# Routed experts on Trainium2: the round counts of an expert group as one packed word, extra rounds as nested branches, packed expert lists

## The chip, the cores and the metric

The kernel runs on one core of one Trainium2 chip. The metric is the device time of one execution in microseconds. Three runs of the kernel before took 1653.17, 1653.27 and 1659.96 us; the median is 1653.27 us. The profiled execution took 1655.41 us, of which the profile's span covers 1653.7 us; the rest lies around it.

## The reference, cut to what matters

Two transformer blocks run one after the other on 256 tokens of width 1024. Each ends in routed experts, and only these are touched by the change. The first has 32 experts, two for each token; the second has 64 experts, eight for each token. All experts have width 256. All weights are float32.

```python
# first block: 4 groups of 8 experts; the best group, then its best two experts
g_top = jnp.argmax(g_logits, axis=-1)
e_in = jnp.take_along_axis(e_logits, g_top[:, None, None], axis=1)[:, 0]
e_val, e_loc = lax.top_k(e_in, TOP_K)
e_w = jax.nn.softmax(e_val, axis=-1) * g_w[:, None]
# for each expert, on the tokens that chose it:
hb = jax.nn.silu(xb @ w_gate[e]) * (xb @ w_up[e])
return (hb @ w_down[e]).astype(F32) * wt[:, None]

# second block: the best 4 of 8 groups, then the best 8 experts of these
g, u = jnp.split(jnp.einsum('td,edf->tef', tc, w_gu), 2, axis=-1)
routed = jnp.einsum('tef,efd->td', jax.nn.silu(g) * u * gc[..., None], w_down)
```

Which tokens an expert gets, and how many, is known only when the kernel runs.

## The kernel before, in words

**Groups, rounds and jobs.** Experts are sorted by their number of tokens, and four of them form a group: two from the busy end of the order and two from the other end. The first layer has NQ = 8 groups, the second 16. A job is 32 tokens of one expert, and a round is four jobs, which lie in four blocks of 32 rows of TensorE. Each group has one round in which every expert of it has a job. If a pair of the group has an expert with more than 32 tokens, extra rounds follow in which only this pair has jobs, two each: n2 extra rounds for the first pair, n3 for the second. The counts come from the routing, which VectorE works out on the chip.

**A round on TensorE** (`one` in `moe_pe`): the gate/up matmuls (L321, two instructions of each kind for each call, since float32 takes two), the gathering of tokens for the next round by one-hot matrices (`pick`, L280), the sum of the last round's outputs into the accumulators (`combine`, L289), the columns of the slots (L270), two transposes (L333), a second `pick`, and the down matmuls (L344). ScalarE and VectorE take silu, product, copies and the next one-hot matrices (`onehot`, L214 to L223) between these. In the first round of a group, TensorE waits for the four experts' gate/up weights (L297) and down weights (L301).

**The order of rounds on TensorE** is written out by hand, group by group (I call one group's share of this a turn). Register loads (`value_load`) read small integers from the list `lst` in memory on the chip. L102 (`window_end`) loads the number of rounds up to this group. After the group's first round, L353 loads n2, a branch (L356) goes past the extra rounds if it is zero, and otherwise a loop of four passes (L357) runs the round where the pass is below n2 (L358). The same follows for n3, with a load of n3 at L353 and one more of n2 at L355. A register load shows in the trace as TENSOR_LOAD, FUSED_REGOPS and SEQ_ASSERT, a branch as COMPARE_BRANCH, all on TensorE's sequencer (PEldq).

```python
for i in range(m.NQ):
    g = window_end(pe, m, i - 1) if i else 0
    one(g, i, (0, 1, 2, 3), True)
    for h, which in enumerate(((0, 1, 0, 1), (2, 3, 2, 3))):
        n = pe.value_load(...L_N + 2 * i + h...)
        if h: g = pe.value_load(...L_N + 2 * i...) + g
        with pe.If(n > 0):
            with pe.Fori(0, T // (2 * JOB)) as r:
                with pe.If(n > r): one(r + (g + 1), i, which, False)
```

**The other engines** run the rounds as a loop over a common number of rounds (`rounds`). SyncE issues the weight loads (`moe_sp`): seven slots hold gate/up weights, 2 MB an expert, and four hold down weights, 1 MB an expert. A slot is loaded anew when the rounds of its group are done.

**Lists.** `route_lists_dve` and `route_lists_pe` make six lists of 80 entries, one entry for each round: the experts of its four jobs, and where the jobs of each pair start (L459 to L466). TensorE turns them into rows by six transposes (L387), and VectorE copies 480 numbers to `lst` as integers (L469). `onehot` reads six numbers for each round.

Of the kernel before, what the change touches and what calls it, by code (L numbers as in the profile page):

```python
# [19 lines left out]
I32 = mybir.dt.int32  # L20
# [6 lines left out]
P = 128  # L27
# [183 lines left out]
def moe_dve(dve, m, ev, ps):  # L211
    def onehot(g):

        first = [dve.value_load(m.lst[0:1, bass.ds(g + (4 + h) * JOBS, 1)], min_val=0, max_val=2 * T - JOB) for h in range(2)]  # L214
        for j in range(PER):
            e = dve.value_load(m.lst[0:1, bass.ds(g + j * JOBS, 1)], min_val=0, max_val=m.E - 1)
            dve.tensor_tensor(m.oneh[:, :, JOB * j:JOB * j + JOB],  # L217
                              m.iota[:, bass.ds(first[j // 2], JOB)].unsqueeze(1).to_broadcast([P, TT, JOB]),
                              m.pos[:, :, bass.ds(e, 1)].to_broadcast([P, TT, JOB]), ALU.is_equal)
# [46 lines left out]
def moe_pe(pe, m, ev, ps):  # L266
# [44 lines left out]

    def one(g, i, which, first):
        at = [PER * i + w for w in which]
# [12 lines left out]
        if not isinstance(g, int):  # L326
# [21 lines left out]

    for i in range(m.NQ):
        g = window_end(pe, m, i - 1) if i else 0  # L350
        one(g, i, (0, 1, 2, 3), True)
        for h, which in enumerate(((0, 1, 0, 1), (2, 3, 2, 3))):
            n = pe.value_load(m.lst[0:1, m.L_N + 2 * i + h:m.L_N + 2 * i + h + 1], min_val=0, max_val=T // (2 * JOB))  # L353
            if h:
                g = pe.value_load(m.lst[0:1, m.L_N + 2 * i:m.L_N + 2 * i + 1], min_val=0, max_val=T // (2 * JOB)) + g  # L355
            with pe.If(n > 0):  # L356
                with pe.Fori(0, T // (2 * JOB)) as r:  # L357
                    with pe.If(n > r):  # L358
                        one(r + (g + 1), i, which, False)
# [7 lines left out]
def route_lists_pe(pe, m, ev, ps):  # L367
# [18 lines left out]
    for i in range(6):  # L386
# [4 lines left out]
def route_lists_dve(dve, m, ev, ps):  # L391
# [38 lines left out]
    dve.tensor_copy(m.lst[0:1, m.L_N:m.L_N + 2 * NQ], m.n[0:1].rearrange("o i h -> o (i h)"))  # L430
# [28 lines left out]
    dve.scalar_tensor_tensor(m.job[:, 0:2], m.dif, third, m.abcd[:, 0:2], ALU.mult, ALU.add)  # L459
    dve.scalar_tensor_tensor(m.job[:, 2:4], m.dif, back, m.abcd[:, 2:4], ALU.mult, ALU.add)  # L460
    dve.tensor_tensor(k, r, k, ALU.subtract)
    dve.drain()
    dve.tensor_scalar(m.job[:, 4:5], k, 2.0 * JOB, -float(JOB), ALU.mult, ALU.add)
    dve.tensor_scalar(m.job[:, 5:6], k, 2.0 * JOB, None, ALU.mult)
    dve.drain()
    dve.tensor_scalar(m.job[:, 4:6], m.job[:, 4:6], ext, float(2 * T - JOB), ALU.mult, ALU.min)  # L466
# [6 lines left out]
def build_program(nc, A, out):  # L473
    ctx = contextlib.ExitStack()
    with ctx:
# [99 lines left out]
        def moe_buffers(prefix, E, most):  # L575
# [10 lines left out]
            m.lst = take("lst", [1, JOBS * 6 + E + 3 * m.NQ]).bitcast(I32)  # L586
            m.L_X, m.L_END, m.L_N = JOBS * 6, JOBS * 6 + E, JOBS * 6 + E + m.NQ
# [6 lines left out]
            m.total, m.end, m.past, m.begun, m.junk = (take(n, [P, m.NQ]) for n in ("total", "end", "past", "begun", "junk"))  # L594
            m.st = take("st", [P, 8])
            m.abcd, m.dif, m.job = take("abcd", [P, PER]), take("dif", [P, 2]), take("job", [P, 6])
# [1517 lines left out]
```

## Time and profile before

| | |
|---|---|
| median of three runs | 1653.27 us |
| the profiled execution | 1655.41 us |
| its span | 1653.7 us |
| TensorE busy | 1278.0 us (77%) |
| VectorE busy | 533.2 us (32%) |
| ScalarE busy | 321.2 us (19%) |
| read from HBM | 399.15 MB, 242 GB/s over the span |
| routed experts, first layer | about 340 to 585 us |
| routed experts, second layer | about 1050 to 1645 us |

How to read it: the busy time of an engine counts only its work, not its sequencer's register loads, branches and waits. In the views, PE is TensorE's matmuls, PEld its weight loads, PEldq and PEq its sequencer, DVE VectorE, ACT ScalarE. "Issue" is time in which an engine waited for nothing that the profile shows, such as its own sequencer. The granted clock of TensorE was 0.875 of its full rate on average.

### The profile page before, as it was taken

The numbers are of one execution on the slowest core, as the hardware profiler recorded it, in microseconds if no ns is written. First come the engines' busy times: TensorE is split into PE (matmuls) and PEld (weight loads), VectorE is DVE, ScalarE is ACT, GpSimd is POOL, SyncE is SP. The second block draws the span as 40 slices with busy tenths as digits, with TensorE's granted clock in tenths as the row PEclk, the third lists the DMA queues.
The fourth block names the chain that finished last, engine by engine and source line by source line (L and its number), as shares of the span: only waits on it lengthen the run. The fifth ranks groups of instructions, "written<-read, shape, count | busy, mean of one in ns | idle before, by whom it ended". The sixth has DMA issues, their size and how long they took to land.

```text
span 1653.7 us, 23849 instructions
## 1 busy us (share of the span) xinstructions
PE 1278.0 (77%) x8269; PEld 675.7 (41%) x8269; DVE 533.2 (32%) x1556; ACT 321.2 (19%) x566; POOL 44.5 (3%) x90
## 2 busy tenths in 40 slices
PE   6998867468746664999479977698999978888645
PEld 4752243333322332864254435344444433344322
DVE  0004132422121113599644414332233332222122
ACT  2114431411100123101352214011111111111000
POOL 1001100200000000000000003000000000000000
PEclk9997767679877877999789997799999999999877
DMA  7548700398999685244000923675888887778993
GB/s 263 184 159 299 251 16 1 118 388 329 421 419 419 270 301 198 96 160 152 0 1 8 348 69 142 255 292 227 326 348 344 350 358 306 286 304 325 427 423 148
DMA packets 87950, 402.32 MB, mean 243 GB/s; under 512 B 10944, under 2 KB 19572, under 8 KB 59136
## 3 DMA queue, kind: packets, MB, share of 16 engines
q1 hardware_dynamic: 86608, 399.70, 61.7%
q8 instruction: 111, 1.82, 0.4%
q10 hardware_dynamic: 816, 0.52, 0.2%
q14 instruction: 31, 0.25, 0.0%
q0 software_dynamic: 384, 0.03, 0.0%
HBM read 399.15 MB, written 1.07 MB: 242 GB/s over the span
## 4 chain that ended last, share of the span: by engine, by line
PE 43%; DMA 8%; issue 4%; DVE 2%; ACT 1%; DVEq 1%; PEldq 1%; PEld 1%; ACTq 0%; SPq 0%
PE ps L1965 17%; PE ps L321 13%; DMA ring<-in_w_exp_gu 5%; PE ps L344 4%; PE ps L280 4%; PE ps L289 2%; DMA big<-in_w_exp_gu 1%; DMA big<-mod 1%; PE ps L797 1%; PE ps L270 0%; PE ps L333 0%; ACT big L1661 0%; DVE big L1780 0%; DVE big L1778 0%; PE ps L2043 0%
## 5 line engine op out<-in xcount | busy, mean ns | idle before, releaser
L321 PE MATMUL ps<-ring,big 128*32 128x512 f32 x2128 | 306.2, 650 | 144.0 <-issue 61.2
L321 PEld LDWEIGHTS ps<-ring,big 128*32 128x32 f32 x2128 | 86.2, 119 | 332.4 <-issue 332.4
L1965 PE MATMUL ps<-ring,big 128*128 128x512 f32 x464 | 202.0, 594 | 2.3 <-ACTq L777 1.1
L321 PE MATMUL ps<-big 128*32 128x512 f32 x304 | 131.0, 657 | 19.7 <-DMA ring<-in_w_up 12.9
L344 PE MATMUL ps<-big 128*32 128x512 f32 x1216 | 138.4, 595 | 0.0
L1965 PEld LDWEIGHTS ps<-ring,big 128*128 128x128 f32 x464 | 87.3, 190 | 110.4 <-issue 107.2
L280 PEld LDWEIGHTS ps<-big 128*128 128x128 bf16 x1920 | 115.4, 99 | 34.6 <-issue 31.9
L280 PE MATMUL ps<-big 128*128 128x128 bf16 x1920 | 125.4, 221 | 1.5 <-ACT big L192 1.5
L201 ACT ACTIVATE big<-ps 128x256 f32<-128x256 f32 x38 | 14.6, 386 | 502.0 <-PE ps L321 502.0
L1766 DVE SCALAR_TENSOR_TENSOR big<-big 128x256 f32<-128x256 f32 x240 | 105.6, 481 | 9.0
L243 DVE TENSOR_TENSOR big<-big,ps 128x256 f32<-128x256 f32 x38 | 16.1, 423 | 276.7 <-ACT big L201 276.7
L217 DVE TENSOR_TENSOR big<-iota,big 128x64 f32 x168 | 37.9, 225 | 202.2 <-issue 202.2
L289 PE MATMUL ps<-parts,slot_tok 128*128 128x512 f32 x304 | 82.6, 415 | 12.4 <-issue 6.8
L192 ACT COPY big<-ps 128x512 f32<-128x512 f32 x80 | 47.0, 588 | 220.2 <-PE ps L280 220.2
L797 PE MATMUL ps<-ident,big 128*128 128x128 f32 x144 | 30.4, 399 | 76.4 <-DVEq L1793 24.8
L1965 PE MATMUL ps<-big,ring 128*128 128x256 f32 x320 | 71.8, 388 | 0.9 <-ACTq L777 0.9
L289 PEld LDWEIGHTS ps<-parts,slot_tok 128*128 128x128 f32 x304 | 56.4, 196 | 24.7 <-issue 14.2
L1965 PEld LDWEIGHTS ps<-big,ring 128*128 128x128 f32 x320 | 62.2, 195 | 9.9 <-ACTq L777 1.1
L344 PEld LDWEIGHTS ps<-big 128*32 128x32 f32 x1216 | 35.7, 110 | 72.2 <-issue 68.2
L797 PEld LDWEIGHTS ps<-ident,big 128*128 128x128 f32 x144 | 27.7, 214 | 80.5 <-DVEq L1240 18.7
L245 DVE COPY big<-ps 128x256 f32<-128x256 f32 x38 | 16.2, 426 | 117.3 <-PE ps L333 117.3
L1346 PE MATMUL ps<-big,ring 128*96 128x256 f32 (+1 forms) x224 | 48.8, 379 | 0.0
(435 smaller groups left out, 1287.6 us busy)
## 6 DMA issues: line engine op xcount, KB each, us to landing
ring<-in_w_exp_gu SPq DMA_DIRECT2D x55, 2048.0 KB, 17.6
big<-in_w_exp_down SPq DMA_DIRECT2D x64, 1024.0 KB, 9.0
big<-in_w_down SPq DMA_DIRECT2D x32, 1024.0 KB, 14.8
ring<-in_w_in SPq DMA_DIRECT2D x15, 2048.0 KB, 8.0
ring<-in_w_gate SPq DMA_DIRECT2D x28, 1024.0 KB, 16.6
ring<-in_w_up SPq DMA_DIRECT2D x28, 1024.0 KB, 19.5
ring<-in_w_ada SPq DMA_DIRECT2D x12, 2048.0 KB, 8.0
big<-in_w_exp_gu SPq DMA_DIRECT2D x9, 2048.0 KB, 18.0
```

Source lines behind the costliest of these rows:

```text
L192: act.copy(m.xsT[:, 4 * r:4 * r + 4, :].rearrange("p a b -> p (a b)"), ps[:, BT, :]).then_inc(ev(m.p + "Te"), 1)
L217: dve.tensor_tensor(m.oneh[:, :, JOB * j:JOB * j + JOB], m.iota[:, bass.ds(first[j // 2], JOB)].unsqueeze(1).to_broadcast([P, TT, JOB]), m ...
L243: dve.tensor_tensor(m.hid, m.sg, ps[:, BG, 256:512], ALU.mult).then_inc(ev(m.p + "hid"), 1)
L245: dve.tensor_copy(m.hidT.rearrange("p a b -> p (a b)"), ps[:, BG, 0:256])
L280: last = pe.matmul(ps[:, BT, c * P:(c + 1) * P], m.tok3[:, part * TT + t, f], m.oneb[:, t, :], start=(part + t == 0), stop=(part == 2 and ...
L289: last = pe.matmul(ps[:, ACC + 2 * t + n, :], m.S[:, t * P:(t + 1) * P], part[:, n * 512:(n + 1) * 512], start=False, stop=True, skip_grou ...
L321: last = pe.matmul(ps[rows, BG, :], m.xsT[:, k, rows], m.gu(m.gu_slot(at[j]), k), start=(k == 0), stop=(k == KC - 1), skip_group_check=True)
L344: last = pe.matmul(ps[rows, BD + n, :], m.hidT[:, k, rows], m.dring[:, at[j] % DOWN_SLOTS, k * D + n * 512:k * D + n * 512 + 512], start=( ...
L797: last = pe.transpose(ps[:, bank0 + c // 2, (c % 2) * T + t * P:(c % 2) * T + (t + 1) * P], src[:, t, c * P:(c + 1) * P], ident[:])
L1346: last = pe.matmul(ps[0:m, g % 4, 0:n], lhs(k), rhs(k), start=(k == 0), stop=(k == KC - 1))
L1766: dve.scalar_tensor_tensor(convT[:, c, :], uT[:, c, k:k + T], dwc[:, c, k:k + 1], convT[:, c, :], ALU.mult, ALU.add)
L1965: last = pe.matmul(bank, lhs(k), rhs(k), start=(k == 0 and start), stop=(k == kk - 1))
```

## The change

1. **Extra rounds on TensorE.** The first extra round of the first pair stands in line within `If(n2 > 0)`; only further ones are in a loop, from pass 1 on, within a second `If(n2 > 1)`. The second pair keeps its loop of four passes, within `If(n3 > 0)`.
2. **One packed word.** n2, n3 and the first round's number of a group are packed into one word (`L_W`), from which TensorE takes all three by shifts and masks. The word of the next group is loaded within this group's first round, behind `combine`. The loads at L102, L353 and L355 go. The word is built on VectorE by two more operations, with a drain and a copy.
3. **Packed lists.** The four experts of a round are packed into one number and the two starts into another: two lists instead of six, two transposes instead of six, and a copy of 160 numbers. `onehot` loads two numbers and takes the rest by shifts and masks on VectorE's sequencer.

```diff
@@ moe_dve, onehot
-        first = [dve.value_load(m.lst[0:1, bass.ds(g + (4 + h) * JOBS, 1)], min_val=0, max_val=2 * T - JOB) for h in range(2)]
+        packed = dve.value_load(m.lst[0:1, bass.ds(g, 1)], min_val=0, max_val=2 ** 24 - 1)
+        chunks = dve.value_load(m.lst[0:1, bass.ds(g + JOBS, 1)], min_val=0, max_val=255)
         for j in range(PER):
-            e = dve.value_load(m.lst[0:1, bass.ds(g + j * JOBS, 1)], min_val=0, max_val=m.E - 1)
+            e = (packed >> (6 * j)) & (m.E - 1)
+            first = ((chunks >> (4 * (j // 2))) & 15) * JOB
@@ moe_pe
+    def word(i):
+        return pe.value_load(m.lst[0:1, m.L_W + i:m.L_W + i + 1], min_val=0, max_val=2 ** 13 - 1)
     def one(g, i, which, first):
...
             combine()
+        if first and i + 1 < m.NQ:
+            following = word(i + 1)
         pe.wait_ge(ev(m.p + "hid"), g + 1)
...
+    following = word(0)
+    more = T // (2 * JOB)
     for i in range(m.NQ):
-        g = window_end(pe, m, i - 1) if i else 0
+        now = following
+        g, n2, n3 = now & 127 if i else 0, (now >> 7) & 7, now >> 10
         one(g, i, (0, 1, 2, 3), True)
-        for h, which in enumerate(((0, 1, 0, 1), (2, 3, 2, 3))):
...
+        with pe.If(n2 > 0):
+            one(g + 1, i, (0, 1, 0, 1), False)
+            with pe.If(n2 > 1):
+                with pe.Fori(1, more) as r:
+                    with pe.If(n2 > r):
+                        one(r + (g + 1), i, (0, 1, 0, 1), False)
+        with pe.If(n3 > 0):
+            with pe.Fori(0, more) as r:
+                with pe.If(n3 > r):
+                    one(r + n2 + (g + 1), i, (2, 3, 2, 3), False)
@@ route_lists_pe
-    for i in range(6):
+    for i in range(2):
@@ route_lists_dve
-    dve.tensor_copy(m.lst[0:1, m.L_N:m.L_N + 2 * NQ], m.n[0:1].rearrange("o i h -> o (i h)"))
+    dve.scalar_tensor_tensor(m.words, m.n[:, :, 1], 8.0, m.n[:, :, 0], ALU.mult, ALU.add)
...
+    dve.scalar_tensor_tensor(m.words, m.words, 128.0, m.begun, ALU.mult, ALU.add)
...
+    dve.drain()
+    dve.tensor_copy(m.lst[0:1, m.L_W:m.L_W + NQ], m.words[0:1, :])
...
-    dve.tensor_copy(m.lst[0:1, 0:6 * JOBS], ps[0:1, BT, 0:6 * JOBS])
+    dve.tensor_copy(m.lst[0:1, 0:2 * JOBS], ps[0:1, BT, 0:2 * JOBS])
```

## Rows read from the trace of the kernel before

**Rows 1.** Page: engines busy (us, share, instructions); DMA queue (packets, MB, share).

```profile
PE 1278.0 (77%) x8269; PEld 675.7 (41%) x8269; DVE 533.2 (32%) x1556; ACT 321.2 (19%) x566; POOL 44.5 (3%) x90
...
q8 instruction: 111, 1.82, 0.4%
```

**Rows 2.** Waits view, TensorE: who waited on what: us in total, times, longest.

```profile
PE ps L321 <- issue: 68.0, 21, 8.2
...
PE ps L321 <- DMA ring<-in_w_up: 45.2, 4, 12.9
```

**Rows 3.** Timeline of TensorE, 540:560 us; then the source view of L297, 555:559 us.

```profile
558.11 2.79 PE L321 MATMUL ps<-ring,big 128*32 128x512 f32 x12 [12.73 <-DMA ring<-in_w_up]
...
L297 PEldq EVENT_SEMAPHORE  x3: 51/51/51, 556.2 to 558.0; - x3
```

**Rows 4.** Windows view: us, busy time by engine (x), PEclk, DMA share, GB/s.

```profile
410.00:560.00 150.00, 92.53 (x802) 42.14 (x798) 27.99 (x95) 11.24 (x20) 0.00 (x0) 0.80 1.01 419
...
1163.00:1525.00 362.00, 315.94 (x3010) 154.68 (x2999) 107.29 (x367) 42.75 (x76) 0.00 (x0) 0.96 0.81 325
...
1215.00:1217.00 2.00, 1.23 (x12) 0.13 (x4) 0.61 (x4) 0.27 (x1) 0.00 (x0) 1.00 0.00 0
```

**Rows 5.** Source views, whole span: duration ns min/median/max, first and last start us.

```profile
L356 PEldq COMPARE_BRANCH  x48: 70/1033/6436, 359.4 to 1637.5; - x48
...
L357 PEldq COMPARE_BRANCH  x52: 86/224/242, 398.5 to 1522.7; - x52
```

**Rows 6.** Source views of L357, L353, 1213:1219 us; timeline of TensorE, 1213:1222.

```profile
L357 PEldq COMPARE_BRANCH  x4: 86/224/238, 1213.6 to 1215.8; - x4
...
L357 PEldq ALU_OP  x4: 32/36/36, 1213.5 to 1215.8; - x4
...
L353 PEldq TENSOR_LOAD <-big x1: 302/302/302, 1216.0 to 1216.0; - x1
...
1218.85 3.64 PE L321 MATMUL ps<-ring,big 128*32 128x512 f32 x32 [2.62 <-issue]
```

**Rows 7.** Source view of L356, in seven short windows of one jump each.

```profile
L356 PEldq COMPARE_BRANCH  x1: 332/332/332, 1180.5 to 1180.5; - x1
...
L356 PEldq COMPARE_BRANCH  x1: 5861/5861/5861, 1358.4 to 1358.4; - x1
...
L356 PEldq COMPARE_BRANCH  x1: 1876/1876/1876, 424.7 to 424.7; - x1
...
L356 PEldq COMPARE_BRANCH  x1: 6436/6436/6436, 1602.4 to 1602.4; - x1
...
L356 PEldq COMPARE_BRANCH  x1: 4236/4236/4236, 1579.7 to 1579.7; - x1
...
L356 PEldq COMPARE_BRANCH  x1: 4741/4741/4741, 1610.2 to 1610.2; - x1
...
L356 PEldq COMPARE_BRANCH  x1: 3371/3371/3371, 1637.5 to 1637.5; - x1
```

**Rows 8.** Chain of what ended last, 1180:1192 us: start us, us, what.

```profile
1184.71 1.39 issue
```

**Rows 9.** Chains of 1360:1376 and 1286:1300 us; timeline of TensorE, 1353:1368.

```profile
1365.40 8.43 PE ps L321 x64
...
1290.81 7.07 PE ps L321 x64
...
1365.40 1.07 PE L321 MATMUL ps<-ring,big 128*32 128x512 f32 x2 [8.08 <-issue]
```

**Rows 10.** Timeline of TensorE 332:342 us; TensorE waits; source view of L214, 333:341.

```profile
332.44 0.96 PE L387 MATMUL ps<-ident,big 80*1 80x80 f32 x6 [5.56 <-DVEq L467]
...
PE ps L270 <- DVEq L223: 13.7, 2, 7.0
...
L214 DVEq TENSOR_LOAD <-big x2: 315/437/559, 334.2 to 335.1; - x2
```

More of the change, by code:

```diff
@@ L212, in onehot @@
     def onehot(g):
-        first = [dve.value_load(m.lst[0:1, bass.ds(g + (4 + h) * JOBS, 1)], min_val=0, max_val=2 * T - JOB) for h in range(2)]
+        packed = dve.value_load(m.lst[0:1, bass.ds(g, 1)], min_val=0, max_val=2 ** 24 - 1)
+        chunks = dve.value_load(m.lst[0:1, bass.ds(g + JOBS, 1)], min_val=0, max_val=255)
         for j in range(PER):
-            e = dve.value_load(m.lst[0:1, bass.ds(g + j * JOBS, 1)], min_val=0, max_val=m.E - 1)
+            e = (packed >> (6 * j)) & (m.E - 1)
+            first = ((chunks >> (4 * (j // 2))) & 15) * JOB
             dve.tensor_tensor(m.oneh[:, :, JOB * j:JOB * j + JOB],
-                              m.iota[:, bass.ds(first[j // 2], JOB)].unsqueeze(1).to_broadcast([P, TT, JOB]),
+                              m.iota[:, bass.ds(first, JOB)].unsqueeze(1).to_broadcast([P, TT, JOB]),
                               m.pos[:, :, bass.ds(e, 1)].to_broadcast([P, TT, JOB]), ALU.is_equal)
@@ L325, in one @@
         pick(0)
-        if not isinstance(g, int):
+        if not (isinstance(g, int) and g == 0):
             pe.wait_ge(ev(m.p + "S"), g)
@@ L347, in one @@
             last.then_inc(ev(m.p + "down"), 1)
+    following = word(0)
+    more = T // (2 * JOB)
     for i in range(m.NQ):
-        g = window_end(pe, m, i - 1) if i else 0
+        now = following
+        g, n2, n3 = now & 127 if i else 0, (now >> 7) & 7, now >> 10
         one(g, i, (0, 1, 2, 3), True)
-        for h, which in enumerate(((0, 1, 0, 1), (2, 3, 2, 3))):
[L353 to L359, printed above, removed]
+        with pe.If(n2 > 0):
[8 more added lines that the diff above has]
+                    one(r + n2 + (g + 1), i, (2, 3, 2, 3), False)
     total = all_rounds(pe, m)
@@ L458, in route_lists_dve @@
     dve.drain()
-    dve.scalar_tensor_tensor(m.job[:, 0:2], m.dif, third, m.abcd[:, 0:2], ALU.mult, ALU.add)
-    dve.scalar_tensor_tensor(m.job[:, 2:4], m.dif, back, m.abcd[:, 2:4], ALU.mult, ALU.add)
+    dve.scalar_tensor_tensor(m.job4[:, 0:2], m.dif, third, m.abcd[:, 0:2], ALU.mult, ALU.add)
+    dve.scalar_tensor_tensor(m.job4[:, 2:4], m.dif, back, m.abcd[:, 2:4], ALU.mult, ALU.add)
     dve.tensor_tensor(k, r, k, ALU.subtract)
     dve.drain()
-    dve.tensor_scalar(m.job[:, 4:5], k, 2.0 * JOB, -float(JOB), ALU.mult, ALU.add)
-    dve.tensor_scalar(m.job[:, 5:6], k, 2.0 * JOB, None, ALU.mult)
+    two = m.job4.rearrange("p (h j) -> p h j", j=2)
+    dve.scalar_tensor_tensor(m.dif, two[:, :, 1], 64.0, two[:, :, 0], ALU.mult, ALU.add)
+    dve.tensor_scalar(k, k, 7.0, 34.0, ALU.min, ALU.mult)
     dve.drain()
-    dve.tensor_scalar(m.job[:, 4:6], m.job[:, 4:6], ext, float(2 * T - JOB), ALU.mult, ALU.min)
+    dve.scalar_tensor_tensor(m.job[:, 0:1], m.dif[:, 1:2], 4096.0, m.dif[:, 0:1], ALU.mult, ALU.add)
+    dve.tensor_scalar(m.job[:, 1:2], k, -1.0, ext, ALU.add, ALU.mult)
     dve.drain().then_inc(ev(m.p + "jobs"), 1)
     dve.wait_ge(ev(m.p + "jobrows"), 1)
-    dve.tensor_copy(m.lst[0:1, 0:6 * JOBS], ps[0:1, BT, 0:6 * JOBS])
+    dve.tensor_copy(m.lst[0:1, 0:2 * JOBS], ps[0:1, BT, 0:2 * JOBS])
     dve.drain().then_inc(ev(m.p + "list"), 1)
@@ L585, in moe_buffers @@
             m.gu_data = lambda slot: ring[:, slot, 0:4096] if slot < RING else gu7
-            m.lst = take("lst", [1, JOBS * 6 + E + 3 * m.NQ]).bitcast(I32)
-            m.L_X, m.L_END, m.L_N = JOBS * 6, JOBS * 6 + E, JOBS * 6 + E + m.NQ
+            m.lst = take("lst", [1, JOBS * 2 + E + 2 * m.NQ]).bitcast(I32)
+            m.L_X, m.L_END, m.L_W = JOBS * 2, JOBS * 2 + E, JOBS * 2 + E + m.NQ
             m.pos = take("pos", [P, TT, E])
@@ L594, in moe_buffers @@
             m.total, m.end, m.past, m.begun, m.junk = (take(n, [P, m.NQ]) for n in ("total", "end", "past", "begun", "junk"))
+            m.words, m.job4 = take("words", [P, m.NQ]), take("job4", [P, PER])
             m.st = take("st", [P, 8])
-            m.abcd, m.dif, m.job = take("abcd", [P, PER]), take("dif", [P, 2]), take("job", [P, 6])
+            m.abcd, m.dif, m.job = take("abcd", [P, PER]), take("dif", [P, 2]), take("job", [P, 2])
             m.own = take("own", [P, PER])
```

1 line of the change is left out of this document (added).

## The prediction

> **What bounds the kernel now.** I read the page first, then TensorE's waits, then the two routed-expert stages (340 to 590 us and 1050 to 1640 us), the only places that the change touches. The page shows TensorE as the busiest engine, 77% [rows 1]. The waits view tells what its idle time ends on: gate/up matmuls (L321) wait 68.0 us on "issue", that is on TensorE's own sequencer, and in four turns 45.2 us on a weight DMA [rows 2]. The DMA label says what came last, not what took long. In the turn that starts at 558.11 us TensorE stood idle for 12.73 us, but its sequencer reached the three waits at L297 only at 556.2 us and had passed the last at 558.0 us [rows 3]: at most 1.8 us were the DMA, the rest was the sequencer.
>
> The stages have two regimes. A turn of the group loop with no extra round is one round, about 17 us of matmuls, against 12 MB of weights; there the DMA share is 1.01 at 419 GB/s (410 to 560 us), and DMA sets the pace. From 1163 to 1525 us, where turns have two rounds each, the DMA share is 0.81 and TensorE is busy for 315.94 of 362 us [rows 4]: TensorE sets the pace, and its idle time counts in full.
>
> Which turns have extra rounds: the loop over them (L357) was entered 13 times (52 loop ends, four to an entry) [rows 5]. By the shortest jumps at L356 (70 to 84 ns, body entered) these are turn 1 of the first layer (n2 = 1) and, in the second, turn 0 (n3 = 1), turn 1 (n2 = 2) and turns 2 to 11 (n2 = 1). Seven turns of the first layer and the last four of the second have none.
>
> **What stands between two rounds.** Turn 5 of the second layer, after its extra round (last matmul issued at 1213.5 us): four loop ends at L357 from 1213.6 us, with the tests at L358 between them; the load of L353 at 1216.0 us and that of L355, each 0.302 us and its register work, 0.65 to 0.72 us in all; a jump over the n3 body, 0.38 us; the load of L102, again 0.65; some 0.4 us of waits; first matmul at 1218.85 us [rows 6]. TensorE had 2.6 us queued when the sequencer left the round, so 5.3 us of sequencer give 2.62 us of idle [rows 6].
>
> **The jump is the dear part.** COMPARE_BRANCH at L356 took 70 to 6436 ns [rows 5], and its place decides. After an extra round the jump took 0.33 to 0.45 us in seven of the ten turns 2 to 11, and 5.8 to 6.0 us in three [rows 7]. In turns without an extra round two jumps follow each other, and the second took 4.2 to 4.7 us every time under full DMA load; the first took 1.9 to 6.4 us [rows 7]. With DMA idle it is less: 3.37 us at 1637.5 us [rows 7]. I read that as code coming from memory: TensorE's instruction queue moves 111 packets, 1.82 MB, 16.4 KB each [rows 1]; for the 28,454 instructions that I count in its program that is 64 B each, 256 to a packet. A round is 316 matmuls and weight loads, some 322 instructions, 1.26 packets. Sorted by their place within a packet, the jumps that don't follow another one fall apart: over one stretch of a quarter to half a packet all are under 0.5 us, over the next all but one, with DMA idle, are 5.7 to 6.4 us; just behind a packet boundary they shrink with the distance (6.0, 4.2, 3.6, 1.9 us). So the next packet is asked for when the one before it is entered, arrives 5.5 to 6.4 us later under DMA load and 3 to 4 us later with DMA idle, and a jump beyond it pays that in full. The bill can come later as well: after a short jump the round at 1181.97 us stops at 1184.71 us for 1.39 us within its matmuls [rows 8]. The Trainium skill says the same in words (Runtime: NRT & Kernel Launch, Instruction fetch mechanics): prefetch is sequential, and a taken branch out of the current two pages waits for a DMA. It speaks against this change, which lengthens the code by a body in each turn.
>
> **The change, part by part (times for the profiled execution, 1655.4 us).**
> 1. Sequencer work removed in a turn with n2 = 1: the loop's empty passes 2.4 us (1213.6 to 1216.0), two loads 1.37, the load of L102 0.64: 4.4 us [rows 6]. Added: four or five register operations; the nearest row is the loop's ALU_OP at 32 to 36 ns, 0.1 us with the gap behind it [rows 6]: 0.4 us (0.2 to 0.8).
> 2. The packed word is loaded within the round, behind combine: 0.66 us in which combine's 8 matmuls (1.9 us) are queued. I cost it at nothing; uncovered it is 24 x 0.66 = 16 us.
> 3. Jumps in such a turn. Before: one, over one body; mean of the ten (7 x 0.38 + 3 x 5.9) / 10 = 2.0 us. After: the extra round runs in line, then a jump over the loop (one body), and at once a jump over the n3 body. The first I leave at 2.0 us. The second is the kind that pairs show: 4.2 to 4.7 us behind 1.3 us of loads, so 5.6 to 6.1 us from the landing of the first; with DMA idle 3 to 4. Here DMA is nearly idle between the end of the round and SyncE's next loads (share 0.00 in 1215 to 1217 us) [rows 4], so about half the turns see each: 4.8 us, bounds 0.35 and 6.1. Net of parts 1 and 3: -4.4 + 0.4 + 4.8 = +0.8 us.
> 4. Idle above 5 us costs clock besides: behind 8.08 us of idle at 1365.40 us the gate/up matmuls take 8.43 us, behind 2.6 us (1290.81) 7.07 [rows 9]: 1.4 us. Three of ten turns have that now, six or so would; and a round that starts late in a packet stops within it. Together +0.7 us. So +1.5 us a turn, ten turns: **+15 us**.
> 5. Second layer, turn 0: +0.5. Turn 1: one empty pass less and no load; -2. Turns 12 to 14: a jump over two bodies and one over one, about 12.5 us beside 13.5 now, but DMA sets the end: 0. Turn 15: DMA idle, loads gone: -1.
> 6. First layer, turn 0: two jumps, 5.0 us in all now, over two bodies and one under full load 6 each; less two saved loads and a test: +4. Turn 1: 0. Turns 2 to 6 lose up to 3 us of sequencer against a slack of some 2 us at the DMA gate [rows 3], and DMA has a backlog then [rows 4]: 0. Turn 7: -0.7.
> 7. Lists: two transposes for six (0.96 us to 0.3), a copy of 160 numbers for 480, two register loads for six ahead of the first picks (about 0.6 us each by the row of L214, against some 0.35 us a job of shifts) [rows 10]; one drain and two small operations more, 0.4 us. TensorE waits for this once a layer (13.7 us in two) [rows 10]: -2 a layer, bounds 0 and -3. In all other rounds VectorE's shorter lists lie beside matmuls and are worth nothing. If they were late, TensorE would show more waits for L223 than these two.
>
> Sum: first layer +4 - 0.7 - 2 = +1.3; second -2 + 0.5 - 2 + 15 - 1 = +10.5; in all +12. Against the median (1653.3, 2.1 us below the profiled execution) that is **1665 us**.
>
> **Rivals.**
> - Jumps come cheap. If a jump in line costs 0.35 us wherever it goes, each of the ten turns gains 4.4 - 0.4 - 0.4 = 3.6 us, 36 in all, and with turn 1, the starts and ends some 44: 1610 us. For it: 7 of 10 single jumps were short. Against: not one second jump under load was. It decides if the second costs less than 4 us. The Trainium skill (Advanced Engine Details and Errata, Control Flow Timing) gives about 108 ns for a compare-and-branch, which would bring this case; no long row here agrees. Chance 0.17.
> - Code comes in strict order and always under load: every skipped packet costs 6 us. Then the pair costs about 11 us for 6.8, +45 in the ten turns, and turns without extra rounds, which now skip 2.5 packets at once, pass the DMA's pace by 3 us in some eight: 1665 + 45 + 24 = 1734. For it: the packets moved (111) equal the whole program, skipped bodies included. Against: one jump beyond the next packet costs no more than one packet. Chance 0.16.
> - The two halves cancel: the second jump lies nearer 3.5 us, since DMA is idle just then. Then the ten turns give 0 +- 8: 1650 to 1660. Chance 0.22.
> - My case, +8 to +40: 0.45.
>
> **Numbers.** Slower by over 0.5% (8 us, about what a measurement can tell here): 0.60; within: 0.19; faster: 0.21 (the first rival and an edge of the third). The range 1632 to 1706 leaves out most of the first rival and of the second.
>
> **What would show it.** Right: L356's successors show two long jumps in a row in turns 2 to 11, 3 to 6 us for the second; the instruction queue moves about 28 packets more; busy times hardly change; TensorE's idle time in turns 2 to 11 grows from 46 us (362 - 316) [rows 4]. Wrong: second jumps under 1 us, or a wait at the new word load. The weakest step is how long a packet takes while DMA is between two loads.

## The result, and the profile after

The changed kernel takes 1674.27 us (median; 1665.59 to 1684.64), the kernel before 1656.49 us in the same session (1644.65 to 1662.24). The ratio is 1.0118, 95% interval 1.0091 to 1.0144: slower by 17.8 us. Forecast were 1665 us and +12. A ratio leaves out executions more than 1.5% above their kernel's fastest; only the last kernel below had any, three of ten, its traced one of 1670.92 us among them. The profiled execution of the changed kernel took 1668.87 us, 1667.1 of it span.

The page of the changed kernel, engines busy and the queue that carries code; these answer [rows 1]:

```profile
PE 1273.8 (76%) x8261; PEld 673.3 (40%) x8261; DVE 532.9 (32%) x1562; ACT 321.4 (19%) x566; POOL 44.5 (3%) x90
...
q8 instruction: 134, 2.20, 0.5%
```

TensorE does the same work in nearly the same busy time. What grew is the code that its queue moved, by 23 packets. Its waits (who waited on what: us in total, times, longest) answer [rows 2] and [rows 10]; L321 has become L328, L270 L272, L223 L225:

```profile
PE ps L328 <- issue: 111.2, 19, 15.5
PE ps L328 <- DMA ring<-in_w_up: 47.8, 4, 13.5
...
PE ps L272 <- DVEq L225: 9.9, 2, 5.1
```

Idle time in front of gate/up matmuls that ends on TensorE's own sequencer went from 68.0 to 111.2 us. The wait for the first round's lists went from 13.7 to 9.9 us.

The windows view of turns 2 to 11 of the second layer (us, busy time by engine, PEclk, DMA share, GB/s), first the kernel before, cut at the first gate/up matmul of turn 2 and of turn 12, then the changed kernel, cut in the same way:

```profile
1141.85:1525.66 383.81, 334.80 (x3161) 163.14 (x3162) 112.67 (x384) 45.00 (x80) 0.00 (x0) 0.95 0.82 330
```

```profile
1141.96:1543.75 401.79, 338.10 (x3160) 163.69 (x3161) 113.59 (x381) 45.01 (x80) 0.00 (x0) 0.92 0.79 320
```

Ten turns take 17.98 us more: 14.7 us are idle time (401.79 - 338.10 = 63.7 against 49.0), 3.3 us are slower matmuls at a lower granted clock. Of the idle time, 18.4 us more lie between rounds (61.33 against 42.95), and the stops within rounds fell from 6.0 to 2.1 us (sums of the gaps in the timelines). The source views of the two jumps in these turns (duration in ns, min/median/max): L366, out of the first half's block behind the in-line round, and L370, over the second half's.

```profile
L366 PEldq COMPARE_BRANCH  x10: 369/3370/4700, 1172.7 to 1533.5; - x10
...
L370 PEldq COMPARE_BRANCH  x10: 3128/5165/6377, 1176.6 to 1537.4; - x10
```

There are two long jumps in a row where there was one. One by one, with the place in a packet of 256 instructions at which L366 stands (counted in the program; its zero is fitted here and is checked below):

| turn | 2 | 3 | 4 | 5 | 6 | 7 | 8 | 9 | 10 | 11 | mean |
|---|---|---|---|---|---|---|---|---|---|---|---|
| place of L366 | .83 | .95 | .07 | .19 | .31 | .44 | .56 | .68 | .80 | .92 | |
| L366, us | 3.65 | 3.81 | 3.54 | 3.20 | 2.45 | 1.13 | 0.43 | 0.37 | 4.70 | 3.63 | 2.69 |
| L370, us | 5.67 | 5.53 | 6.08 | 3.35 | 3.13 | 3.27 | 4.80 | 4.55 | 6.38 | 5.79 | 4.85 |

Both jumps span 1.28 packets. From 0.72 on a jump lands two packets further, and waits; behind a boundary it lands in the next packet, which has only just been asked for, and the wait shrinks with the distance, to nothing at 0.6. In the timeline the end of turn 2 looks like this (start us, us, instruction, idle time before it and its releaser):

```profile
1182.80 1.04 PE L328 MATMUL ps<-ring,big 128*32 128x512 f32 x1 [7.32 <-issue]
```

7.32 us of idle time, where the same place had 2.63 us before.

That the jumps wait for code can be read directly, since the traces hold the times of the code queue's packets. The DMA view of the changed kernel in the time of two jumps (queue: packets that started, MB, share), first L366 at the end of turn 2 (1172.74 to 1176.39 us), then L370 behind it (1176.56 to 1182.23 us):

```profile
q1 hardware_dynamic: 29, 0.21, 13.8%
q8 instruction: 1, 0.02, 2.2%
```

```profile
q1 hardware_dynamic: 250, 1.92, 94.0%
q8 instruction: 1, 0.02, 1.1%
```

The code packet starts 1.0 us after the first jump and 3.4 us after the second, takes 1.3 and 1.0 us, and each jump ends 1.4 us after it has landed. The second jump is longer because SyncE's weight loads run by then. From 300 us on, the twelve traces of this text have 336 branches on TensorE that last over 2.2 us. A code packet lands within every one of them, and the branch ends 1.3 to 2.0 us after the last one (in 316 of them 1.3 to 1.6 us). Of the 802 branches under 0.6 us, 780 have none.

### The profile page after: what moved, and what is told of

Same layout as the page of the kernel before. It is cut to its first block, busy times and chain, and to the rows that moved or that the text cites. A ratio compares the mean times of both kernels' runs of the same rounds, so it can differ in the third digit from the quotient of the medians.

```text
span 1667.1 us, 23346 instructions
## 1 busy us (share of the span) xinstructions
PE 1273.8 (76%) x8261; PEld 673.3 (40%) x8261; DVE 532.9 (32%) x1562; ACT 321.4 (19%) x566; POOL 44.5 (3%) x90
## 4 chain that ended last, share of the span: by engine, by line
PE 44%; issue 6%; DMA 5%; DVE 3%; ACT 2%; DVEq 1%; PEld 1%; SPq 0%; PEldq 0%; ACTq 0%
PE ps L1985 16%; PE ps L328 13%; PE ps L353 5%; PE ps L282 4%; DMA ring<-in_w_exp_gu 3%; PE ps L291 3%; DMA big<-in_w_exp_gu 1%; PE ps L272 1%; PE ps L817 1%; PE ps L342 0%; DMA big<-mod 0%; SPq L1564 0%; DMA posi<-in_positions 0%; DVE big L1800 0%; DVE big L1798 0%
## 5 line engine op out<-in xcount | busy, mean ns | idle before, releaser
L328 PE MATMUL ps<-ring,big 128*32 128x512 f32 x2128 | 312.2, 670 | 154.6 <-issue 95.8
L328 PEld LDWEIGHTS ps<-ring,big 128*32 128x32 f32 x2128 | 88.2, 122 | 349.3 <-issue 346.3
L328 PE MATMUL ps<-big 128*32 128x512 f32 x304 | 132.2, 662 | 28.9 <-issue 15.5
L353 PE MATMUL ps<-big 128*32 128x512 f32 x1216 | 138.4, 595 | 0.0
L353 PEld LDWEIGHTS ps<-big 128*32 128x32 f32 x1216 | 35.7, 110 | 72.2 <-issue 68.2
L328 PEld LDWEIGHTS ps<-big 128*32 128x32 f32 x304 | 30.9, 121 | 53.4 <-issue 52.5
```

What stands on the lines that cost most here:

```text
L328: last = pe.matmul(ps[rows, BG, :], m.xsT[:, k, rows], m.gu(m.gu_slot(at[j]), k), start=(k == 0), stop=(k == KC - 1), skip_group_check=True)
L353: last = pe.matmul(ps[rows, BD + n, :], m.hidT[:, k, rows], m.dring[:, at[j] % DOWN_SLOTS, k * D + n * 512:k * D + n * 512 + 512], start=( ...
```

## The experiments

Ten kernels ask three things: which part of the change costs, what a long jump waits for, and whether it can be had without. Ratios are to the kernel before, which ran beside each.

**Only the packed lists on VectorE.** The kernel before with this part alone:

```diff
-        first = [dve.value_load(...) for h in range(2)]
+        packed = dve.value_load(m.lst[0:1, bass.ds(g, 1)], ...)
+        chunks = dve.value_load(m.lst[0:1, bass.ds(g + JOBS, 1)], ...)
-    for i in range(6):
+    for i in range(2):
         last = pe.transpose(...)
```

> Kernel before with the packed expert lists on VectorE alone; TensorE's loads, loops and branches are as before, its code is 16 instructions shorter. Theory (a jump pays for a code packet that has not come): the list stages give 2 us each, 4 us in all; besides, all of the second layer's code moves by 0.06 packet, so that after extra rounds the long jumps of 5 to 6 us stand in turns 7 and 8 and no longer in turn 9: another 5 us. 9 us faster than before, ratio 0.994. Rival (jumps cost what they cost by the load on the DMA queues, not by their place): long jumps stay in turns 7, 8 and 9, 4 us faster, 0.998.

Measured: 0.9966 (0.9945 to 0.9986), 1647.58 us. The lists bring 5.6 us (2.3 to 9.1). In the traces the stage from the matmuls ahead of the transposes (L382, in the changed kernel L396) to the first pick is 2.07 us shorter in the first layer of the changed kernel, and 1.66 in the second; the interval holds that sum. The long single jumps came at the ends of turns 6, 7 and 8 (5.57, 5.86, 5.73 us), where the kernel before has them at 7, 8 and 9: still three, so no gain there. My count of where they would go was off by one turn.

**Only the in-line copy.** The kernel before with the changed kernel's nested branches, but each count loaded where it is used:

```diff
+        n2 = count(i, 0)
         with pe.If(n2 > 0):
-            (loop over four passes)
+            one(g + 1, i, (0, 1, 0, 1), False)
+            with pe.If(n2 > 1): (loop over three passes)
+        n3 = count(i, 1)
+        n2 = count(i, 0)
         with pe.If(n3 > 0): ...
```

> Kernel before with the in-line copy of the first extra round and the nested branch alone; the counts are loaded as before, lists as before. Theory: in turns 2 to 11 of the second layer the three empty passes go (2.4 us), but a second jump comes, from which the two loads between the jumps hide 1.3 us: first jumps 28 us in all, second ones 32 us, against 20 us of single jumps before, so +40 - 24 = +16 us there, +7 us in the first layer (turn 0 and its DMA), -1 in turn 1: 20 to 25 us slower, ratio 1.013. Rival (the sequencer's work is what counts, a jump is 0.4 us): 10 x 2.0 us faster, ratio 0.988.

Measured: 1.0202 (1.0177 to 1.0227), 1688.82 us, +33 us. The rival, that removed passes are a gain, falls, and the theory gave too little. In turns 2 to 11 (source views) the first jump takes 2.69 us on average and the last 2.89:

```profile
L360 PEldq COMPARE_BRANCH  x10: 371/2994/5376, 1189.8 to 1550.1; - x10
...
L366 PEldq COMPARE_BRANCH  x10: 1682/2919/4362, 1196.5 to 1553.9; - x10
```

Here two loads stand between the jumps, 1.3 us [rows 6], and the second jump is 2.0 us shorter than the changed kernel's 4.85. The loads also lengthen a turn, so the places in the packet differ too.

**Only the word and the lists.** The changed kernel without the copy:

```diff
         with pe.If(n2 > 0):
-            one(g + 1, i, (0, 1, 0, 1), False)
-            with pe.If(n2 > 1):
-                with pe.Fori(1, more) as r:
+            with pe.Fori(0, more) as r:
```

> The changed kernel without the in-line copy: the packed word, read ahead, and the packed lists stay, both pairs have the loop of four passes again, one body each. Theory: each of the ten turns loses two loads and the one of L102 and gains 0.4 us of shifts, -1.6 us; code is as long as before, one jump after an extra round, long (5 to 6 us) in turns 5 and 6 alone by its place; lists -4 us. In all -16 - 5 - 4 = -25 us against before, ratio 0.985. Rival (the word's read ahead costs TensorE within the round): 0.66 us in each of 24 turns back, ratio 0.995. Rival (the in-line copy is no matter): like the changed kernel, 1.01.

Measured: 0.9763 (0.9739 to 0.9787), 1615.73 us. Better than any case expected. So the copy, put on top of this, costs 1.0118 / 0.9763 = 1.036, some 59 us, almost twice the 33 us that it costs alone. The windows view of its turns 2 to 11 says where the unexpected part is:

```profile
1141.69:1492.24 350.55, 325.43 (x3160) 166.19 (x3161) 114.72 (x385) 45.04 (x80) 0.00 (x0) 0.99 0.89 361
```

33.3 us less than before, of which 23.9 us are idle time (25.1 against 49.0) and 9.4 us are faster matmuls at a granted clock of 0.99 instead of 0.95. The second part I had left out. At the ends of these turns the kernel before has three gaps of 8 us and seven of 2.6 to 2.8 us; here six of ten are under 2 us and the longest is 3.9. The windows view of the kernel before shows that even the shorter gaps can cost clock, and need not. These are the first 64 gate/up matmuls behind a gap of 2.71 us and behind one of 2.62 us:

```profile
1254.60:1263.37 8.77, 8.77 (x66) 2.90 (x66) 2.73 (x4) 0.00 (x0) 0.00 (x0) 0.81 1.01 419
1290.81:1297.88 7.07, 7.07 (x65) 2.43 (x66) 2.75 (x4) 0.00 (x0) 0.00 (x0) 1.00 1.01 425
```

**Loops that end at the count.** The same, without the empty passes:

```diff
-            with pe.Fori(0, more) as r:
-                with pe.If(n2 > r):
-                    one(r + (g + 1), i, (0, 1, 0, 1), False)
+            with pe.Fori(0, n2) as r:
+                one(r + (g + 1), i, (0, 1, 0, 1), False)
```

> As e3_word, but the loops run to the count itself, with no empty passes and no test inside. Theory: 2.4 us of empty passes go too, so the jump comes earlier after its packet was asked for and part of it comes back: jumps about 29 us in the ten turns against 20 before, sequencer -40 us, lists -4, turn 1 -3: about -38 us against before, ratio 0.977; long jumps (over 3 us) in turns 3, 4, 9, 10, 11. Rival (empty passes hide the fetch in full): same as e3_word.

Measured: 0.9713 (0.9690 to 0.9736), 1607.92 us. The empty passes took 2.4 us of sequencer in a turn [rows 6], but ten turns gain only 350.55 - 343.16 = 7.4 us by their removal: the jump over the second half's block, 1.45 us on average with them, is 2.67 us without (its places in the packet moved as well). They had covered part of the fetch.

**A gap between the jumps.** The changed kernel with 3.9 us of loads of no use:

```diff
+        for _ in range(6):
+            word(i)
         with pe.If(n3 > 0):
```

> The changed kernel with six more loads of the count word (0.65 us of sequencer each, 3.9 us in all, 21 instructions) between the first half's branch and the second half's, in every turn. Theory (the second jump waits for a packet that arrives at its own time, whatever the sequencer does meanwhile): in the second layer's turns 2 to 11 the second jump falls from 4.86 us to about 1.2 us (each value of the changed kernel less 3.9, not under 0.35), the two together stay, and the time stays within 8 us of the changed kernel's, ratio to before 1.010 to 1.018. Rival (the jump has a price of its own, paid from when it issues): the second jump stays near 4.9 us, each of the 24 turns is 3.9 us longer less what the DMA hides in the first layer and turns 12 to 15, some +45 us, ratio 1.035 to 1.045.

Measured: 1.0372 (1.0333 to 1.0411), 1712.96 us. The time is the rival's, the trace is neither's alone. Two jumps over the second half's block (L372), at the ends of turns 2 and 4, in the source view:

```profile
L372 PEldq COMPARE_BRANCH  x1: 6232/6232/6232, 1189.7 to 1189.7; - x1
...
L372 PEldq COMPARE_BRANCH  x1: 439/439/439, 1279.0 to 1279.0; - x1
```

In six of the ten turns the second jump is 0.34 to 0.50 us: the loads cover its whole wait. These are the turns whose first jump waited (2.89 to 3.36 us), so that the packet behind its landing place was asked for before the gap. In the other four the first jump took 0.36 to 0.45 us and the second, which lands two packets on, 5.75 to 6.74 us: the gap doesn't help, since nothing asks for that packet before the jump. The packet times agree. In the six turns a code packet lands between the two jumps, and none within the second. In the four one lands between them too, but another starts within the second, 3.4 to 4.4 us after its start, beside weight loads:

```profile
q1 hardware_dynamic: 317, 2.34, 94.4%
q8 instruction: 1, 0.02, 1.0%
```

(DMA view, 1189.65 to 1195.88 us.) The loads also lengthen a turn's code and so moved every jump to another place. The windows view of the ten turns:

```profile
1148.38:1570.16 421.78, 345.09 (x3160) 165.03 (x3161) 113.11 (x380) 45.04 (x80) 0.00 (x0) 0.90 0.75 302
```

Against the changed kernel the turns are 20.0 us longer, not 39: 13.0 us of idle time (76.7 against 63.7) and 7.0 us of clock, 0.90 against 0.92. So about two thirds of the added sequencer time lay within waits for code. The rest of the 1.0372 came outside these turns, where I had counted on cover from the DMA. A fixed price of a jump is refuted; my figure for the time was wrong.

**Code moved, nothing else.** The kernel before with one alignment ahead of the second layer's lists:

```diff
+    if m.E == 64:
+        pe.addr_align(256, offset=147, max_nops=0)
     pe.wait_ge(ev(m.p + "jobs"), 1)
```

> The kernel before, with nothing but an alignment of TensorE's code ahead of the second layer's lists, which moves all code behind it by 0.35 of a 256-instruction packet. Theory (a jump of 1.28 packets waits when it starts in the last quarter of a packet, since its landing place is then two packets on): the long single jumps over the second half, which were in turns 7, 8 and 9 (5.8 to 6.0 us), go to turns 2, 3, 10 and 11; turns 4 to 9 show 0.33 to 0.6 us. Time 1650 to 1665 us. Rival (something of turns 7 to 9 itself, such as their experts or the loads under way, makes the jump long): they stay in turns 7, 8 and 9.

Measured in one execution: 1653.84 us. The long jumps left turns 7, 8 and 9, as only the theory says, but went to 5, 6 and 7:

```profile
L356 PEldq COMPARE_BRANCH  x1: 5781/5781/5781, 1285.6 to 1285.6; - x1
...
L356 PEldq COMPARE_BRANCH  x1: 5663/5663/5663, 1327.3 to 1327.3; - x1
...
L356 PEldq COMPARE_BRANCH  x1: 5681/5681/5681, 1368.6 to 1368.6; - x1
...
L356 PEldq COMPARE_BRANCH  x1: 351/351/351, 1409.9 to 1409.9; - x1
```

I had miscounted where the lists stand in the program: the alignment moved the code by 0.75 of a packet, not 0.35. With the right count the jumps at the ends of turns 5, 6 and 7 start at 0.96, 0.84 and 0.72 of a packet, and all others, at 0.61 and below, are short. That needs no fitted zero, since the alignment sets it, and it confirms the one used in the table above.

**Fewer weights beside the code.** The changed kernel, where the second layer loads a quarter of each expert's weights from its second turn on:

```diff
+            if getattr(m2, "light", False):
+                eng.dma_start(m2.gu_data(slot)[:, 0:1024], ...[:, 0:1024]).then_inc(sem, 16)
+                return
```

> The changed kernel, but from its second turn on the second layer loads only a quarter of each expert's gate/up and down weights, so that its result is not the reference's; TensorE's instructions are the same. Theory (a packet of code comes through the same DMA engines, behind weight packets): with the DMA engines mostly idle a packet comes in 3 to 3.5 us, so the second jumps of the second layer's turns 2 to 11 fall from 4.86 to about 3 us and none is over 4, the jumps of turns 12 to 15 from 5.5 to 6.7 down to about 3 us each; those turns, no longer held by loads, fall from 30 to about 23 us. Rival (the wait is a fixed price of a refill, whatever the DMA engines do): second jumps stay at 4.5 to 6 us.

Measured in one execution: 1642.21 us; the DMA share of the ten turns is 0.27 instead of 0.79. The source views of its second jumps in turns 2 to 11, and of both jumps in turns 12 to 15:

```profile
L373 PEldq COMPARE_BRANCH  x10: 2862/3851/4605, 1187.0 to 1528.2; - x10
...
L367 PEldq COMPARE_BRANCH  x4: 3440/3705/3957, 1548.8 to 1620.6; - x4
...
L373 PEldq COMPARE_BRANCH  x4: 3142/3394/3922, 1552.4 to 1624.7; - x4
```

In turns 12 to 15 the pair fell to 3.1 to 4.0 us each; the changed kernel, under full load, has 6.1 to 6.5 and 5.5 to 5.7 us there in turns 12 to 14. In turns 2 to 11 the second jump fell from 4.85 to 3.73 us on average, not to 3, and four were over 4.1 us: weights account for about a quarter of that wait. In two of the four, turns 8 and 9 (4.61 and 4.54 us), the code queue moved two packets within the jump. The ten turns are 22 us shorter (379.57 us).

**A hint for the jump.** The kernel of the fourth experiment, with the jump over the second half's block announced at the head of the extra round:

```diff
             with pe.Fori(0, n2) as r:
+                here = pe.mark_branch_hint_location()
                 one(r + (g + 1), i, (0, 1, 0, 1), False)
-        with pe.If(n3 > 0):
+        pe.br_eq(n3, 0, on_true=name + "_end", on_false=name + "_body").branch_hint(here)
```

> e4_count (the packed word read ahead, loops that end at the count, no in-line copy) with one thing added: at the head of the first half's extra round the code hints that the jump over the second half's block will be taken, some 16 us before that jump. Theory (a jump waits because the packet of its landing place has only just been asked for, or not yet): in the second layer's turns 2 to 11 of e4_count that jump lasted 3.13, 3.89, 3.39, 0.36, 1.09, 1.62, 2.75, 3.25, 3.53 and 3.64 us; with the packet asked for 16 us earlier all ten are 0.3 to 0.6 us. TensorE's idle time between these turns falls from 11 us in all to about 0, and with fewer slow gate/up matmuls the ratio to the kernel before goes from 0.971 to about 0.962. Rival (the jump itself is dear, or the hint does nothing): the jumps stay at 3 us and the ratio at 0.971. Third: the hint fetches a packet that is thrown out again before the jump; then waits of 3 us and more stay, and code traffic grows by some ten packets.

Measured: 0.9706 (0.9661 to 0.9751), 1599.59 us; not told apart from 0.9713. The source views of a jump that lands two packets on, at the end of turn 4, first without the hint and then with it:

```profile
L367 PEldq COMPARE_BRANCH  x1: 3392/3392/3392, 1237.1 to 1237.1; - x1
```

```profile
L370 PEldq COMPARE_BRANCH  x1: 388/388/388, 1231.2 to 1231.2; - x1
```

Without the hint the four jumps from 0.77, 0.83, 0.92 and 0.99 of a packet took 3.4 to 3.9 us; with it the three from 0.79, 0.92 and 0.94 took 0.37 to 0.39. Jumps just behind a boundary waited as before: 2.84 and 2.88 us at 0.22 and 0.21, 3.57 and 3.54 at 0.08 and 0.07. The hint fetches a packet that the order of the code would skip; it does not hasten the next one. The page has 106 packets on the code queue instead of 110. My "all ten" was wrong, and the position in the packet stayed as the thing to set. That is the next experiment.

**Hint and place.** Each turn of the second layer starts at instruction 55 of a packet, so that the hinted jump starts at 0.80:

```diff
         now = following
+        if m.E == 64:
+            pe.addr_align(256, offset=55, max_nops=0)
```

> e5_hint with one thing added: each turn of the second layer starts at instruction 55 of a 256-instruction packet, so that a turn takes 4.00 packets instead of 3.86 and the jump over the second half's block starts at 0.80 of a packet in every turn. In e5_hint that jump lasted 0.37 to 0.39 us where it started at 0.64, 0.79, 0.92 and 0.94 of a packet, and 0.49 to 0.76 at about 0.4 to 0.5, 2.04, 2.88, 2.84 and 3.54 at 0.35, 0.21, 0.22 and 0.07. Theory (position within the packet, with the hint, decides): all ten jumps of turns 2 to 11 last under 0.6 us, the idle time of TensorE between these turns falls from about 7 us in all to under 2, and the ratio to the kernel before is about 0.965. Rival (the waits belong to the turns, not to the place in the packet): long jumps stay in turns 2, 3, 8, 9 and 10 and the ratio at 0.971. Third: the branch over the padding costs more than it gives, 0.3 us and more in each of 16 turns; then the jumps are short and the ratio still 0.970 or above.

(In the text above "0.49 to 0.76 at about 0.4 to 0.5" should read 0.76 us at 0.49.) Measured: 0.9656 (0.9632 to 0.9679), 1593.85 us, the fastest kernel here: by the ratios 57 us under the kernel before and 76 under the changed one. The source view of the hinted jump, then the windows view, turns 2 to 11:

```profile
L372 PEldq COMPARE_BRANCH  x10: 367/378/408, 1158.2 to 1453.5; - x10
```

```profile
1128.06:1456.99 328.93, 319.24 (x3164) 163.27 (x3157) 114.14 (x384) 45.04 (x80) 0.00 (x0) 1.00 0.93 384
```

All ten jumps are short, the clock is full. Idle time is 9.7 us, not the 2 expected; TensorE's waits in this stretch say what holds it now:

```profile
PE ps L328 <- DMA ring<-in_w_exp_gu: 7.1, 8, 1.3
PE ps L353 <- DMA big<-in_w_exp_down: 1.0, 2, 0.5
PE ps L328 <- DMA big<-in_w_exp_gu: 0.5, 1, 0.5
```

In this stretch nothing waits for the sequencer any more; the weights are the bound, at a DMA share of 0.93. Turns 12 to 14 have no extra round and so no hint: their jumps over the second half's block take 7.40 to 7.64 us, against 5.57 to 7.14 without the fixed place.

**Hints in the changed kernel.** Two, both at the head of the in-line copy:

```diff
         with pe.If(n2 > 0):
+            here = [pe.mark_branch_hint_location() for _ in range(2)]
             one(g + 1, i, (0, 1, 0, 1), False)
-            with pe.If(n2 > 1):
+            pe.br_lt(n2, 2, on_true=..., on_false=...).branch_hint(here[0])
...
-        with pe.If(n3 > 0):
+        pe.br_eq(n3, 0, on_true=..., on_false=...).branch_hint(here[1])
```

> The changed kernel with two hints at the head of each in-line copy: that the jump out of the first half's block is taken, and the one over the second half's. Nothing else is changed. In e5_hint a hint took the wait from jumps that land two packets on and from no others. Theory: the first jumps of turns 2, 3, 10 and 11, which land two packets on (3.65, 3.81, 4.70, 3.63 us), fall to about 0.4 us; the second jump of the same turns lands one packet further and still waits some 3 to 6 us; the others stay. That is 14 us of jump time less in four turns, of which some comes back in the second jumps: ratio to before 1.000 to 1.010. Rival (both hinted packets are kept): both jumps are short in all turns, and the ratio falls to 0.98. Second rival: the second hint displaces the first, all first jumps stay as they were, ratio 1.012.

Measured: 0.9991 (0.9951 to 1.0032): level with the kernel before, and a little below the 1.000 to 1.010 that the theory gave. The first jumps that land two packets on, at 0.82, 0.92 and 0.95 of a packet, take 0.37 to 0.38 us; in the changed kernel the four at 0.80 to 0.95 took 3.63 to 4.70. (The added instructions moved the places to turns 9, 2 and 10.) The second jumps, hinted as long ahead, are still 3.07 to 5.84 us. One hint at a time took effect; whether the second is dropped or its packet thrown out wasn't tried. The source views of the two jumps in turns 2 to 11:

```profile
L368 PEldq COMPARE_BRANCH  x10: 367/759/5042, 1192.8 to 1526.8; - x10
...
L376 PEldq COMPARE_BRANCH  x10: 3068/3762/5842, 1193.4 to 1532.0; - x10
```

The ten turns of each kernel side by side, from the windows and source views:

| kernel | ten turns, us | TensorE idle, us | clock | first jump, mean us | last jump, mean us |
|---|---|---|---|---|---|
| before | 383.81 | 49.0 | 0.95 | - | 2.03 |
| changed | 401.79 | 63.7 | 0.92 | 2.69 | 4.85 |
| in-line copy alone | 396.57 | 57.8 | 0.93 | 2.69 | 2.89 |
| changed with gap | 421.78 | 76.7 | 0.90 | 2.08 | 2.77 |
| changed, few weights | 379.57 | 44.1 | 0.95 | 2.15 | 3.73 |
| changed with two hints | 377.14 | 44.5 | 0.95 | 1.79 | 4.10 |
| without copy | 350.55 | 25.1 | 0.99 | - | 1.45 |
| loops to the count | 343.16 | 19.3 | 0.99 | - | 2.67 |
| and hint | 335.79 | 16.3 | 1.00 | - | 1.72 |
| and aligned turns | 328.93 | 9.7 | 1.00 | - | 0.38 |

## Why the prediction was right, and where it was not

1. **Removed and added sequencer work** (part 1): the direction stands. Taken away without the copy, the loads alone, forecast at 16 us in ten turns, come with 23.9 us less idle time; 5.8 us of it are shorter jumps (1.45 us on average against 2.03).
2. **The word read ahead costs nothing** (part 2): right. The source view of its load in the changed kernel shows all 24, and TensorE has no new wait behind it:

```profile
L316 PEldq TENSOR_LOAD <-big x24: 298/306/494, 335.9 to 1611.3; - x24
```

3. **The jumps** (part 3). The second was put at 4.8 us and measured 4.85, with both kinds that were forecast: three at 3.13 to 3.35 us, the rest above 4.5. The first was left at 2.0 and is 2.69; I put that down to places behind a boundary, where the empty passes and loads no longer give the packet time. By the jumps the net is +1.5 us in a turn; the idle time between rounds grew by 1.8 (18.4 / 10), not by 0.8. This term was mis-sized, by 10 us in all. What I had not seen is that the removed sequencer work was partly cover: without the empty passes the same jump takes 2.67 us instead of 1.45, and behind the gap it falls from 4.85 to 2.77.
4. **Clock and stops within a round** (part 4): +0.7 us a turn forecast, 7 us in ten turns. Measured are 3.3 us of slower matmuls and 3.9 us less of stops within rounds, so -0.6. The stops went the other way than forecast. For the clock, the kernel before had already lost more than I counted: its matmuls take 334.80 us in these turns, against 319.24 at a clock of 1.00, and only 6.2 of these 15.6 us lie behind its three gaps of 8 us. "Above 5 us" was too simple a line, as the two rows of the experiment without the copy show. The errors of parts 3 and 4 nearly cancel: 18.0 us against 15. That is luck.
5. **Second layer besides**: from the first gate/up matmul of turn 0 to that of turn 1 +3.5 us (35.39 against 31.88) for +0.5; turn 1 +1.2 (50.85 against 49.63) for -2; turns 12 to 14 and on to the start of turn 15 -3.7 (87.68 against 91.41) for 0; turn 15 -1.0 for -1. Turns 0 and 1 fell short for the reason of point 3: a jump of turn 0 rose from 0.42 to 4.05 us and that of turn 1 from 0.36 to 3.33 us. In turns 12 to 14 DMA sets the pace, as forecast. That it was done sooner fits with more weights having been moved by then: turns 2 to 11 moved some 128.6 MB (401.79 us at 320 GB/s) against 126.7, and 1.9 MB are about 4 us at the 424 GB/s of turns 12 to 14 (an estimate from the windows views).
6. **First layer**: from the first gate/up matmul to the load at L77 behind the last round, 242.41 us against 234.14: +8.3 for a forecast of +3.3. In turn 0 both jumps are long, as forecast, if below the 6 us each that I gave them; the source views of L364 and L370:

```profile
L364 PEldq COMPARE_BRANCH  x1: 4647/4647/4647, 352.7 to 352.7; - x1
...
L370 PEldq COMPARE_BRANCH  x1: 5650/5650/5650, 357.5 to 357.5; - x1
```

   10.3 us for 5.0, and the turn is 5.0 us longer (25.04 against 20.08 us). Its first gate/up matmuls take 9.24 us at a clock of 0.76, where they took 7.08 at 1.00; I had no term for that. The other 3.3 us I counted at nothing, in turns whose end DMA sets. Turn 5 shows what was wrong with that: it is 3.4 us longer (33.24 against 29.82), and at its end, in the timelines of the changed kernel and of the kernel before, the sequencer has taken the place of the DMA:

```profile
526.99 1.08 PE L328 MATMUL ps<-ring,big 128*32 128x512 f32 x3 [15.52 <-issue]
```

```profile
526.79 1.07 PE L321 MATMUL ps<-ring,big 128*32 128x512 f32 x3 [11.64 <-DMA big<-in_w_up]
```

   All kernels with the copy are 4.5 to 12.2 us above the kernel before over this stretch (238.7 to 246.3 us), and those without it take 232.2 to 234.9 us, so it is the copy.
7. **Lists**: -2.07 and -1.66 us up to the first pick for -2 each; right, and late lists show nowhere. In the first layer 1.2 us of it is given back at once, since the second pick takes 2.74 us at a clock of 0.50, for 1.55 us at 1.00.
8. **The sum.** From the matmuls ahead of the transposes (L396, before L382) to the load at L77 the changed kernel takes 7.3 us more (262.61 against 255.29), and in the second layer, from the same matmuls to the end, 16.3 us more (630.42 against 614.13): 23.6 us for a forecast of 12. The two traces' spans differ by only 13.4, because in the rest of the program, which the change hardly touches, the changed kernel's trace is 10.2 us shorter. Such stretches vary from trace to trace: the first one takes 317.7 to 326.4 us in the twelve. How much of the 23.6 us the medians hold isn't known. The forecast has the mechanism, but it is nearer to the 17.8 us between the medians than its terms are to the traces, and that is luck as well.

**The rivals.** Cheap jumps: refuted, no second jump is under 3.1 us. Strict order, every skipped packet fetched: refuted. The pair of jumps takes 7.5 us on average, not 11, the time is 60 us short of that rival's 1734, and of the changed program's 36,042 instructions (my count), 140.8 packets, 134 were moved. The cancelling halves needed a second jump of 3.5 us; three of ten were that short. The forecast's own case holds, and both the 23.6 us of the traces and the 17.8 us between the medians are within its +8 to +40.

The in-line copy is the whole loss: without it, the rest of the change is a gain (0.9763). Its 1.26 packets in each turn buy nothing that the loop didn't give, and put a second landing place behind the first.

## What to carry to other kernels

Look up how long the taken jumps on the bounding engine last, one by one, before branches are rearranged there: a long one is a wait for code, and removing other sequencer work ahead of it gives back only a part of that work's time. Keep blocks that are usually skipped short or few, put no second far jump straight behind a first, and read values ahead within the work, which here was worth 2.0% (0.9763 against 0.9966), shorter jumps and a higher clock included. Where a far jump stays, a hint set a round ahead together with a fixed place in the packet removed its wait.

## What the runs showed of the hardware

- A taken jump over a block on TensorE lasts 0.33 to 0.50 us if its packet is there. If not, it ends 1.3 to 2.0 us after a packet of the code queue has landed (all 336 branches over 2.2 us, in twelve traces). From the start of such a jump to that of its packet it took 1.0 us with the DMA engines nearly idle (share 0.16 in the first jump of turn 2) and 3.4 to 4.4 us beside weight loads (share 0.95 in the second). Whole jumps mostly took 2.9 to 4.6 us with few weights under way (share 0.27 over the ten turns), and 4.2 to 7.6 us under full load where the packet had just been or was yet to be asked for.
- A hint made jumps that land two packets on short (3.4 to 3.9 us to 0.37 to 0.39), left those that land in the next packet, and a second one set with it had no effect. In the kernel with two hints one test within the empty passes of turn 1 took 8.64 us, where it otherwise takes 0.2 to 0.4. The code queue moved three packets within it, and it ended 1.4 us after the third had landed, so it too waited for code; that the hints had displaced a packet of the loop is likely but not shown.
- The granted clock of the ten turns goes with TensorE's idle time: 1.00 at 9.7 and 16.3 us, 0.99 at 19.3 and 25.1, 0.95 at 49.0, 0.92 at 63.7, 0.90 at 76.7 us. A gap of 2.71 us was followed by matmuls at 0.81, gaps of 2.62 and 2.81 us by matmuls at 1.00, each of 8 us by slower ones. The clock has two levels, 1.2 and 2.4 GHz, so 0.95 is a mean over time at either.
